# A routed-expert loop: token rows fetched by an indirect DMA two groups ahead, in place of one-hot products, and a fifth weight buffer

## The reference

```python
s = sigmoid(h @ w_router); biased = s + b_router
# the best 4 of 8 groups of experts, and among their experts the best 6
combine = sum(one_hot(eidx, 64) * (s[eidx] / sum(s[eidx]) * 2.5))
gu  = einsum("td,edf->tef", h, w_expert_gu)              # (64, 1024, 512)
act = silu(gu[..., :256]) * gu[..., 256:] * combine[..., None]
routed = einsum("tef,efd->td", act, w_expert_down)       # (64, 256, 1024)
gs = h @ w_shared_gu
f = routed + (silu(gs[..., :256]) * gs[..., 256:]) @ w_shared_down
x = x + gate_f * rmsnorm(f, g_post_ffn)
```

## Time and profile before

| | us |
|---|---|
| median of 3 runs (lowest, highest) | 807.18 (805.46, 815.96) |
| the profiled execution: its time | 809.28 |
| the profiled execution: its span | 807.4 |
| PE busy | 750.2 (93%) |
| DVE busy | 364.7 (45%) |
| ACT busy | 224.7 (28%) |

### The profile page before, as it was taken

The page is one execution under the profiler, slowest core; times in us unless marked ns, Lnnn a source line. Parts: engine busy times, 40 slices in busy tenths (PEclk is TensorE's granted clock), DMA queues, the critical chain, the costliest instruction groups (busy, mean ns, idle before and its releaser), DMA issues.

```text
span 807.4 us, 12707 instructions
## 1 busy us (share of the span) xinstructions
PE 750.2 (93%) x4893; PEld 454.1 (56%) x4893; DVE 364.7 (45%) x899; ACT 224.7 (28%) x382; POOL 77.3 (10%) x41
## 2 busy tenths in 40 slices
PE   1689899998988999999999999999999999999985
PEld 1579788786855455444555544455554445555442
DVE  2177010176075675454444544445544444445443
ACT  3045223473235022222222222222222222222232
POOL 4024443510401100000000000000000000000000
PEclk9889999999999999999999999999999999999997
DMA  9996866406575448999999999999999999999712
GB/s 315 386 355 235 301 227 242 147 2 77 212 305 216 157 162 358 366 368 422 412 411 427 397 369 428 414 404 427 403 428 426 401 425 410 358 425 428 308 54 80
DMA packets 47249, 256.09 MB, mean 317 GB/s; under 512 B 6224, under 2 KB 8880, under 8 KB 30416
## 3 DMA queue, kind: packets, MB, share of 16 engines
q1 hardware_dynamic: 39344, 247.47, 76.4%
q10 hardware_dynamic: 7040, 6.54, 3.4%
q0 software_dynamic: 800, 1.20, 0.5%
HBM read 253.07 MB, written 2.13 MB: 316 GB/s over the span
## 4 chain that ended last, share of the span: by engine, by line
PE 81%; DMA 6%; DVE 5%; ACT 3%; SPq 1%; issue 1%; ACTq 1%; POOL 1%; DVEq 0%
PE psum L1801 24%; PE psum L1830 12%; PE psum L1756 10%; PE psum L1773 9%; PE psum L484 4%; PE psum L486 4%; PE psum L485 4%; PE psum L1765 3%; DMA w_gu<-in_w_ada 3%; DMA w_gu<-in_w_in 2%; PE psum L1681 2%; PE psum L1474 2%; PE psum L1698 1%; DMA w_gu<-in_w_expert_gu 1%; SPq L548 1%
## 5 line engine op out<-in xcount | busy, mean ns | idle before, releaser
L1801 PE MATMUL psum<-w_gu,hgT 128*32 128x512 f32 (+1 forms) x1344 | 198.1, 594 | 1.1 <-ACT hgT L855 0.7
L1331 DVE TENSOR_TENSOR f_acc<-f_acc,psum 128x512 f32<-128x512 f32 x168 | 115.4, 688 | 49.8 <-PE psum L1773 49.7
L1801 PEld LDWEIGHTS psum<-w_gu,hgT 128*32 128x32 f32 (+1 forms) x1344 | 60.7, 119 | 135.7 <-issue 134.7
L1830 PE MATMUL psum<-w_dn,actT 128*32 128x512 f32 (+1 forms) x672 | 102.1, 596 | 0.0
L1322 DVE TENSOR_TENSOR y_lo<-psum,y_hi 128x1024 fp32r<-128x1024 f32 x28 | 34.3, 1225 | 106.7 <-ACT y_hi L867 106.7
L479 POOL TENSOR_TENSOR w_lo<-w_gu,w_hi 128x2048 fp32r<-128x2048 f32 x13 | 59.8, 4606 | 137.0 <-ACT w_hi L629 137.0
L1756 PE MATMUL psum<-h_hi,onehot 128*128 128x512 f32 x174 | 71.2, 409 | 0.0
L1773 PE MATMUL psum<-y_hi,onehotT 128*128 128x512 f32 x168 | 70.4, 419 | 0.0
L1756 PE MATMUL psum<-h_lo,onehot 128*128 128x512 f32 x174 | 68.0, 391 | 0.0
L1773 PE MATMUL psum<-y_lo,onehotT 128*128 128x512 f32 x168 | 66.0, 393 | 0.0
L850 ACT ACTIVATE hg<-psum 128x512 f32<-128x512 f32 x58 | 34.7, 599 | 99.2 <-PE psum L1756 99.2
(11 more groups left out here) (279 smaller groups left out, 917.1 us busy)
## 6 DMA issues: line engine op xcount, KB each, us to landing
w_gu<-in_w_expert_gu SPq DMA_DIRECT2D x64, 2048.0 KB, 13.0
w_dn<-in_w_expert_down SPq DMA_DIRECT2D x64, 1024.0 KB, 10.1
w_gu<-in_w_ada SPq DMA_DIRECT2D x12, 2048.0 KB, 14.0
w_gu<-in_w_in SPq DMA_DIRECT2D x5, 2048.0 KB, 17.1
w_gu<-in_w_out SPq DMA_DIRECT2D x2, 2048.0 KB, 10.9
bc<-mod_rows ACTq DMA_DIRECT2D x6, 512.0 KB, 13.0
w_gu<-in_w_shared_gu SPq DMA_DIRECT2D x1, 2048.0 KB, 7.7
out<-x SPq DMA_DIRECT2D x3, 512.0 KB, 2.6
```

The lines of the kernel that those rows point to most:

```text
L1331: v.tensor_tensor(dst, dst, bank(5 + n), ALU.add).then_inc(f_added, 1)
L1801: ins = t.matmul(bank(2)[rows, :], hgT[:, c, rows], w_gu[s][:, c, :], start=(c == 0), stop=(c == NC - 1), tile_position=(0, rows.start))
L1830: ins = t.matmul(bank(3 + n)[rows, :], actT[:, j, rows], w_dn[s][:, j, 512 * n:512 * (n + 1)], start=(j == 0), stop=(j == 1), tile_positio ...
```

## The change

- The rows of `h` are stored in DRAM (`h_rows`, from ACT's queue) as they are made, in place of being split; `hp` has three buffers.
- For each group `slots` (PE, three products with 6 or 8 columns) finds the token of each slot and its weight. DVE turns the tokens into integers (`tokens_of`), and GpSimd issues one indirect DMA for 128 rows of 4 KB, 512 KB, for the group two ahead, into one of two buffers `hg`. A slot without a token reads row 0. All 28 groups do this. The product `gather` and its evacuation by ACT are gone.
- The turned one-hot matrix is now made by DVE, by comparing the token of each slot with a row of token numbers, and not by PE.
- The SBUF that `h_hi` and `h_lo` had is a fifth weight buffer, so that SP loads n + 5; `FIXED` is 6. The number of groups stays 28.
- `combine` of a group moves into the gate and up of the next group, a piece behind each of the last five of its eight steps; the sixth piece follows the transpositions of `hg`.
- The gather for a group that may follow the loop is no longer made in the last group.

```diff
-FIXED = 4
+BUFFERS = 5
+RING = 4
+FIXED = 6
...
+        token_w = at("token_w", [P, NT, 8], cursor[0] + 1024, F32R)
+        iota3 = at("iota3", [P, NT, P], cursor[0] + 1120)
...
+        onehot = at("onehot", [P, NT, P], BC + 15360, F32R)
+        onehotT = [at("onehotT0", [P, NT, P], BC + 16896, F32R), at("onehotT1", [P, NT, P], BC + 18432, F32R)]
...
+        w_gu.append(at("w_gu4", [P, NC, 2 * F], Z))
+        w_dn.append(at("w_dn4", [P, 2, D], Z + 16384))
...
+        hp = [at("hp0", [P, NC, P], Z + 28672), at("hp1", [P, NC, P], Z + 40960), at("hp2", [P, NC, P], Z + 45056)]
+        hg = [at("hg0", [P, NC, P], Z + 32768), at("hg1", [P, NC, P], hT_at + 8192)]
...
+        h_dram = nc.dram_tensor("h_rows", [T, D], F32).ap()
...
-            return n % SLOTS, PRE + 1 + n // SLOTS
+            return n % BUFFERS, 1 + n // BUFFERS
         first_load = [sum(len(g) for g in PLAN[:k]) for k in range(GROUPS + 1)]
         def refills(k):
-            return [n + SLOTS for n in range(first_load[k], first_load[k + 1]) if n + SLOTS < NE]
+            return [n + BUFFERS for n in range(first_load[k], first_load[k + 1]) if n + BUFFERS < NE]
...
-            for e in range(SLOTS):
-                sp.wait_ge(gu_used[e], PRE)
+            for e in range(BUFFERS):
+                if e < SLOTS:
+                    sp.wait_ge(gu_used[e], PRE)
+                else:
+                    sp.wait_ge(mT_done, NT)
                 sp.dma_start(w_gu[e][:, :, :], w_egu[e]).then_inc(gu_in[e], 16)
...
-            def high_part(i):
+            def rows_out(i):
                 a.wait_ge(hp_ready, i + 1)
-                a.activation(h_hi[:, i, :, :], hp[:, :, :], ACT.Copy).then_inc(hi_ready, 1)
+                a.dma_start(h_dram[P * i:P * i + P, :], hp[i][:, :, :].rearrange("p c q -> p (c q)")).then_inc(h_out, 16)
...
-            def hg_evac(p):
-                for n in range(2):
-                    a.wait_ge(gathered, p * 2 + (n + 1))
-                    a.activation(hg[:, n, :], bank(n), ACT.Copy).then_inc(hg_ready, 1)
...
+                if k + 1 < GROUPS:
+                    hgT_evac(k + 1)
+                actT_evac(k + (NT + 1))
+                y_high(s_last, uses)
...
-            def low_part(i):
-                v.wait_ge(hi_ready, i + 1)
-                v.tensor_tensor(h_lo[:, i, :, :], hp[:, :, :], h_hi[:, i, :, :].bitcast(F32), ALU.subtract)\
-                    .then_inc(lo_ready, 1)
...
+            def tokens_of(p, par, ring, parts):
+                v.wait_ge(slots_done, p + 1)
+                found = bank(par, 0, 8)
+                v.tensor_copy(idx_u[ring][:, :], found[:, 0:1]).then_inc(idx_ready, 1)
+                own.add(v.tensor_copy(idx_f[:, ring:ring + 1], found[:, 0:1]))
                 for column, (first, end) in enumerate(parts):
                     q = slice(first, end)
-                    ins = v.tensor_reduce(wsl[q, par:par + 1], tiles[q, :, P + 2 * column:P + 2 * column + 2], AX.XY, ALU.add)
+                    ins = v.tensor_reduce(wsl[q, ring:ring + 1], found[q, 2 + 2 * column:4 + 2 * column], AX.X, ALU.add)
                     if column < len(parts) - 1:
                         own.add(ins)
                 ins.then_inc(wsl_ready, 1)
+            def onehot_T(par, ring):
+                own.wait()
+                v.tensor_scalar(onehotT[par][:, :, :], iota3[:, :, :], idx_f[:, ring:ring + 1], None, ALU.is_equal)\
+                    .then_inc(ohT_ready, 1)
...
+                if k + 2 < GROUPS:
+                    tokens_of(k + 2, k % 2, (k + 2) % RING, parts_of(k + 2))
                 if k == 0:
                     over_table()
-                group_output(k, k % 2)
-                onehot_T(k + 1, (k + 1) % 2, parts_of(k + 1) if k + 1 < GROUPS else HALVES)
+                else:
+                    f_add(k - 1, range(5))
+                group_act(k, k % RING)
+                if k:
+                    f_add(k - 1, [5])
+                onehot_T(k % 2, k % RING)
+                if k + 3 < GROUPS:
+                    make_onehot(k + 3)
                 low_y(k)
...
+            def gather(par, ring):
+                g.indirect_dma_start(hg[par][:, :, :].rearrange("p c q -> p (c q)"), None, h_dram[:, :],
+                                     bass.IndirectOffsetOnAxis(ap=idx_u[ring][:, :], axis=0)).then_inc(hg_in[par], 16)
+            g.wait_ge(h_out, 16 * NT)
             wait_chunk(g, "s")
-            for m in range(2):
-                row_from_dram(g, gate_rows[:, m, :], m, 10, gate_rows_in)
+            for k in range(GROUPS):
+                if k >= 2:
+                    g.wait_ge(hgT_done, 2 * (k - 1))
+                g.wait_ge(idx_ready, k + 1)
+                gather(k % 2, k % RING)
+                if k == 4:
+                    g.wait_ge(gate_out, 32)
+                    for m in range(2):
+                        row_from_dram(g, gate_rows[:, m, :], m, 10, gate_rows_in)
...
+            def slots(p, par, owners):
+                t.wait_ge(oh_ready, p + 1)
+                end = 2 + 2 * owners
+                for i in range(NT):
+                    ins = t.matmul(bank(par, 0, end), onehot[:, i, :], token_w[:, i, 0:end],
+                                   start=(i == 0), stop=(i == NT - 1))
+                ins.then_inc(slots_done, 1)
...
+            t.wait_ge(ident_ready, 2 * NT)
+            slots(0, 0, len(PLAN[0]))
             transposes(3)
+            slots(1, 1, len(PLAN[1]))
             sh_down(2)
...
-            def onehot_T(par, owners):
-                width = P + 2 * owners
-                for i in range(NT):
-                    ins = t.matmul(bank(2, (P + 8) * i, (P + 8) * i + width), onehot[par][:, i, :], ident_w[:, i, 0:width],
-                                   start=True, stop=True)
-                ins.then_inc(ohT_done, 1)
-            def gather(par, n, parts):
-                every = [(i, part) for i in range(NT) for part in (h_hi, h_lo)]
-                for k in parts:
-                    i, part = every[k]
-                    ins = t.matmul(bank(n), onehot[par][:, i, :], part[:, i, 4 * n:4 * n + 4, :],
-                                   start=(k == 0), stop=(k == len(every) - 1))
-                if every[k] == every[-1]:
-                    ins.then_inc(gathered, 1)
-            def gathered_T(p, n):
-                t.wait_ge(hg_ready, p * 2 + (n + 1))
-                for c in range(4):
-                    ins = t.transpose(bank(n, P * c, P * c + P), hg[:, n, P * c:P * c + P], ident)
-                ins.then_inc(hgT_done, 1)
+            def gathered_T(p, par, landed, found):
+                t.wait_ge(wsl_ready, found)
+                t.wait_ge(hg_in[par], landed * 16)
+                for n in range(2):
+                    for c in range(4):
+                        ins = t.transpose(bank(n, P * c, P * c + P), hg[par][:, 4 * n + c, :], ident)
+                    ins.then_inc(hgT_done, 1)
...
+            def gate_up(p, tiles, uses, outputs=None):
+                for s, n in uses:
+                    t.wait_ge(gu_in[s], (n + gu_base(s)) * 16)
                 for c in range(NC):
                     for s, rows, last in tiles:
                         ins = t.matmul(bank(2)[rows, :], hgT[:, c, rows], w_gu[s][:, c, :],
                                        start=(c == 0), stop=(c == NC - 1), tile_position=(0, rows.start))
                         if c == NC - 1 and last:
                             ins.then_inc(gu_used[s], 1)
-                if after_gu is not None:
-                    after_gu()
-                t.wait_ge(oh_ready, p + 2)
-                nxt = (par + 1) % 2
-                t.wait_ge(y_ready, p + 1)
-                gather(nxt, 0, (0, 1, 2))
-                combine(p, 0, nxt)
-                gather(nxt, 0, (3, 4, 5))
-                combine(p, 1, nxt)
-                gather(nxt, 1, (0, 1, 2))
-                combine(p, 2, nxt)
-                gather(nxt, 1, (3, 4, 5))
-                combine(p, 3, nxt)
-                transposes(p + (NT + 1))
-                combine(p, 4, nxt)
-                gathered_T(p + 1, 0)
-                combine(p, 5, nxt)
-                gathered_T(p + 1, 1)
-                onehot_T(nxt, next_owners)
+                    if outputs is not None and c >= 3:
+                        outputs(c - 3)
...
+                t.wait_ge(hgT_ready, 2 * k + 2)
+                if k + 2 < GROUPS:
+                    slots(k + 2, k % 2, len(PLAN[k + 2]))
+                def outputs(c):
+                    if c == 0:
+                        t.wait_ge(y_ready, k)
+                        t.wait_ge(ohT_ready, k)
+                    combine(k - 1, c, (k - 1) % 2)
+                gate_up(k, tiles, uses, outputs if k else None)
+                if k == 0:
+                    over_rows()
+                if k + 1 < GROUPS:
+                    gathered_T(k + 1, (k + 1) % 2, (k + 1) // 2 + 1, min(k + 3, GROUPS))
+                if k:
+                    outputs(5)
```

(19 more changed lines are left out.)

217 lines of the change are left out of this document (102 added, 115 removed).

## The result

The median went from 807.25 us to **813.62 us** (20 runs each; 800.08 to 815.96 before, 810.05 to 818.58 after). The ratio is **1.0093, with a 95% interval of 1.007 to 1.0116**: slower, by about 6 us and less than 2%, where 805.7 was forecast. The profiled execution had 813.65 us for a span of 811.8, 4.4 more than the span of before.

What follows compares the result with a forecast made beforehand. The bound moves from PE to the DMA stream, 18.3 us a group: 284.3 + 425.9 + 38.0 + 2.5 = 750.7, two last groups to 782.8, plus 23.1 gives span 805.9, scaled to median 805.7 (predicted 806). Range 793 to 823.

Steps and rivals of the forecast that it cites:

- What bounds the kernel: Loop: PE sets 17.67 us a group, the DMA limit is 16.9; with the rows DMA needs 18.3 and becomes the bound.
- the start of group 26: Late in the loop: its gate and up waits for load 61; 284.3 + 425.9 + 38.0 + 2.5 = 750.7.
- Rate: DMA stream up to load 61: 181.4 MB at 426 GB/s take 425.9 us.
- Gathers: Row loads in the stream: 1.46 us each, bounds 1.23 and 2.77; 26 of them take 38.0 us.
- From last byte to semaphore: End of load 61: 2.5 us between its last byte and its semaphore.
- PE's group: PE's work per group in the loop: 16.4 us, 1.3 less than 17.67; 18 if nothing overlapped as hoped.
- the uncovered path: Each group, from gate and up to down, no longer hidden behind the gather: 3.2 us, of which PE fills some 1.5.
- rival 2: Loop: PE stays the bound, by the uncovered path or a clock falling in waits; 18.4 us a group gives 823; chance 0.10.
- The end: After the last down product: 23.1 us, including 3.3 of issue, the same as before.
- The start: Before the loop: last shared product ends at 284.2, first gather lands near 284.5, group 0 begins at 287, not 288.88.
- Rivals 1 and 3: 1: loop gathers dear, 2.77 us each, to 840, chance 0.15; 3: stream at 434, gathers 1.23 us, 792, chance 0.13.
- Rival 4: After the loop: a table or token order makes further groups necessary, since two more experts are fixed; chance 0.02.

Runs made afterwards that it cites:

- before_bytes: Kernel before, plus a plain 512 KB load from GpSimd's queue that nothing reads, for each of 27 groups; 830.69 us, ratio 1.0291.
- block_combine: Changed kernel with the five combine pieces in one block behind gate and up, not woven in; 814.42 us, ratio 1.0077.
- no_rows: Changed kernel without the row gathers from group 2 on, later groups reusing the rows of groups 0 and 1; 785.5 us, ratio 0.9741.
- four_buffers: Changed kernel with four weight buffers in place of five; 854.55 us, ratio 1.0577.
- distinct: Changed kernel with each slot's row number set to its partition number, so every gather reads 128 different rows; 812.99 us, ratio 1.0099.
- plain_act: Changed kernel with plain loads of fixed rows from ScalarE's hardware queue replacing the indirect gathers from group 2 on; 814.2 us, ratio 1.0091.
- plain_pool: Changed kernel with plain loads of fixed rows from GpSimd's software queue replacing the indirect gathers; 811.84 us, ratio 1.0071.
- late_gates: Changed kernel with the 1.05 MB of gate rows loaded when the last group's tokens are transposed, not behind the fifth gather; 812.61 us, ratio 1.0077.
- skip_late: Changed kernel with rows of empty slots not fetched and the gate rows loaded late; 803.82 us, ratio 0.9976.

## Why the prediction was right in its mechanism and wrong in its sign

**What bounds the kernel: right.** The limit of the DMA engines was said to stand 0.8 us above PE's 17.67. `before_bytes` shows how near it is, `block_combine` that PE no longer matters, and `no_rows` that PE alone would need 17.1 us a group. After, the loop takes 471.1 / 26 = 18.1 us a group.

**The three effects, now sized.** Each size is that of one edit with the rest of the change in place, so they can't be added up. The bytes of the rows cost 26.4 us of loop (471.1 against 444.7 in `no_rows`), the fifth buffer gives 38 to the changed kernel (`four_buffers`), and PE's work per group is 0.6 us shorter (17.67 to 17.1). The loop that comes out is 11.1 us longer than before, and 1.9 at the start, 0.4 in the last two groups and 4.4 at the end take part of it back. The prediction credited the fifth buffer with 7.4 us, the early load alone. Its sum still came near because its model of the stream assumed a queue that never empties, and that is what the buffer gives; that the new order would need it for that wasn't seen.

**The step that failed: the start of group 26, 750.7 forecast and 758.1 measured.** Four terms of it were off.
- *Rate.* 426 GB/s was taken from one window of before; the stream ran at 421 over 284.4 to 758. For 181.4 MB that is 430.9 us, not 425.9: 5.0 more.
- *Gathers.* The price of 1.46 us each was too high, and the lower bound was right: `distinct`, `plain_act` and `plain_pool` agree that rows cost their bytes, 0.524 MB / 421 = 1.24 us. For 26 that is 32.4 and not 38.0: 5.6 less.
- *Gate rows.* Before, 1.05 MB of them moved while there was room in the queue; now they stand in the full stream. They were forgotten: 2.5 us at 421, of which `late_gates` found 1.6.
- *From last byte to semaphore.* With these three, everything ordered up to load 61 and 26 gathers, 196.0 MB, is moved at 284.4 + 196.0 / 0.421 = 750.0. Group 26 began 8.1 us later, and 2.5 had been allowed, from the quickest load of before. This is the failed term, **5.6 us**. By 758 the engines had moved 421 x 473.6 = 199.4 MB: 3.4 MB of later loads before load 61 was whole.

Why is a load whole so late? One-microsecond windows at the end of the stream, of the changed kernel and then of before:

```profile
769.00:770.00 1.00, 1.00 (x10) 0.33 (x3) 0.42 (x1) 0.19 (x1) 0.00 (x0) 1.00 0.93 385
770.00:771.00 1.00, 1.00 (x11) 0.91 (x9) 0.61 (x2) 0.37 (x2) 0.00 (x0) 1.00 0.60 254
...
772.00:773.00 1.00, 0.53 (x6) 0.16 (x8) 0.75 (x2) 0.38 (x1) 0.00 (x0) 1.00 0.20 82
...
776.00:777.00 1.00, 1.00 (x8) 0.34 (x6) 0.00 (x0) 0.60 (x1) 0.00 (x0) 1.00 0.06 25
```

```profile
761.00:762.00 1.00, 1.00 (x8) 0.82 (x8) 1.00 (x2) 0.47 (x2) 0.00 (x0) 1.00 1.03 442
762.00:763.00 1.00, 1.00 (x9) 0.84 (x7) 0.78 (x2) 0.69 (x2) 0.00 (x0) 1.00 0.62 262
763.00:764.00 1.00, 1.00 (x13) 0.40 (x16) 0.86 (x4) 0.42 (x1) 0.00 (x0) 1.00 0.06 16
```

Before, the share falls from 1.03 to 0.06 in two microseconds: all 16 engines end together. After, it takes from 770 to 777, and from 773 on a share of 0.06 to 0.08 is one engine of sixteen. The engines have drifted apart by some 7 us.

The trace holds the same for every load, as each raises its semaphore by 16 in 16 separate signals. Load 61 sent its first at 750.06, the fifteenth at 754.29 and the last at 757.98, and PE began group 26 0.14 later, as the chain shows. The first is at the turn of its bytes, 750.0; the mean of the sixteen is 752.2, which the 2.5 allowed would have covered; what was missed is the wait for the slowest. From first to last signal, in us, of the expert weights' loads that landed in each stretch (median), and of load 61:

| | 300 to 400 | 500 to 550 | 650 to 700 | load 61 |
|---|---|---|---|---|
| before | 1.3 | 2.0 | 2.2 | 1.9 |
| `before_bytes` | 1.9 | 2.4 | 2.1 | 2.6 |
| `four_buffers` | 2.0 | 1.7 | 2.2 | 1.8 |
| changed | 2.9 | 5.6 | 8.0 | 7.9 |

So the drift is there at 750, and it grows along the loop, in the changed kernel and not in those with four buffers, whose share stayed at 0.94 to 0.99. For load 61 it is 6.6 in `plain_act`, 6.7 in `plain_pool` and 8.4 in `distinct`, and 4.4 in `no_rows`, whose share was 0.98. That a queue that never runs empty is what lets it grow fits these runs; why one engine is slower than the others isn't shown. The Trainium skill ("DMA: Bandwidth & Descriptors", section "Latency and other measured facts") has two engines that are usually slower and gives as its best guess the software queue's rings; `plain_act`, whose row loads from group 2 on are on a hardware queue, has the same tail, so here that cause does not carry it. No experiment took the drift away without other changes, so what the loop would gain without it is an estimate: if all sixteen kept their mean, 757.98 - 752.2 = 5.8 us at load 61.

**PE's group: 17.3 us, not 16.4.** The changes from row-tiled to full products were mis-sized. A piece of combine inside gate and up takes 0.67 and not 0.47, and each step of four products behind it 1.01 and not a share of the 6.9 (0.86). Gate and up with its pieces, 300.74 to 311.02, took 10.3 and not 6.9 + 4 x 0.47 + 0.5 = 9.3; `slots` took 0.43 and not 0.3; the uncovered path, 311.02 to 313.96, took 2.9 and not 3.2. In the loop this cost nothing, as `block_combine` shows. In the last two groups, which wait for no load once the first of them has begun, it is 2 x 0.9.

**The clock.** PE's waits do have a price there. After the wait of 3.35 us ahead of group 26 the granted clock was 0.50, the lower of the two levels, for two microseconds, and 32 products took 4.94 us where 3.64 is usual. That is 1.3 us (not every such wait does it: in `skip_late` 32 products behind a wait of 3.85 took 3.64), and with the 1.8 above it makes 3.1, near the 2.9 by which the last two groups missed 32.1. Of rival 2, which named this clock, only so much is true. Where the stream is the bound, such slow products cost nothing, as the next load is late anyway.

**The end: 18.7 us, not 23.1.** It was taken to be unchanged. The six products on `f_acc` took 2.84 us against 5.48 before, at a clock of 1.00 from 795 to 798 where before had 0.50 from 787 to 793. The chain of before:

```profile
787.65 5.48 PE psum L1878 x6
```

That part is luck: in the profiled executions of the eleven kernels with the change they took 2.84 in six and 4.47 to 4.54 in five, `no_rows` and `distinct` among them. The issue time ahead of them was 1.90 and not the 3.33 of the earlier trace rows. It is 2.2 or less in all eleven and 3.45 in `before_bytes`, so it goes with the changed program; why wasn't looked into. These 4.4 us are more than half of the miss in the loop, with the other sign, so the span missed by only 5.9, nearer than the forecast of the loop deserved.

**The start: right.** `sh_down` ended at 284.4 (284.2 forecast), the first transposition followed at 284.72, group 0 at 286.98 (287). The first two gathers landed 4.4 and 4.8 us after their issue (5.4 allowed). The rule from the Trainium skill ("SBUF — State Buffer", section "A bandwidth-pool intuition that's wrong (but worth ruling out)"), which would have put 2.5 us on it, is not seen here.

**The signs asked for.** A first gate and up near 287: yes. A share of 1.0: yes, though at 420 to 427 and not 425 to 430. Waits of 30 to 50 us for `w_gu`: 21.1, as PE itself was slower than forecast. PE busy 60 to 80 us less: 28. Gathers landing in 5 to 10 us: 10.9 in the median, none waited for. Rivals 1 and 3 are refuted: no gather is dear, and the stream did not run at 434. Rival 4 did not come about either: 28 gathers and no group after the loop.

So the sign was lost on the lag of the last loads, which have to wait for the slowest engine: 8.1 us where 2.5 was allowed. The forecast left 1.5 us between the two kernels, as the difference of terms of 5 to 8 us, and such a difference is smaller than the error of each of them.

## What to carry to other kernels

When an engine and the DMA stream are as near to each other as here (17.67 and 16.9 us a group), work taken off the engine and put on the stream as bytes is paid nearly in full, while the gain ends at the stream: weigh bytes before instructions. The number of buffers decides whether the stream runs at its limit: count what may be on order while the largest group holds its buffers, since one more buffer here gave 38 us and one early load would have been 7. Count as well how long a group holds them: a new order of the products can lengthen that while it shortens the group. In a queue that is never empty a load may land well behind its bytes' turn (8 us here at the end of the loop), so look at when the last of its signals comes, and compare versions by a stretch between two events of the loop, not by the span of one execution.

## What the runs showed of the hardware

- An indirect DMA of 128 rows of 4 KB took GpSimd 0.94 us to issue (28 of them) and cost the stream no more than a plain load of the same size: loops of 471.1, 470.3, 470.0 and 469.9 us for the four forms. Rows skipped by its bound don't move: 10.17 MB in place of 15.03.
- One core's DMAs moved 420 to 423 GB/s from 284 to 758, in each of the six versions with five buffers that move the rows of every slot.
- The 16 DMA engines drift apart under a queue that stays full: a load's first and last signals lay 2.9 us apart at 300 to 400 and 8.0 at 650 to 700, against about 2 throughout with four buffers.
- A pair of full products among row-tiled ones cost 0.67 us and 0.15 more in the products behind it, against 0.47 where it stood alone.
